# A two-layer gated attention and convolution trunk: scaling moved ahead of the weights' split, and one convolution tile moved from GpSimd to VectorE

## The reference

```
h = rmsnorm(x);  proj = h @ w_in            # 10 groups of columns
y_a = window_attention(q, k, v, sinks, bias) @ w_attn_out
c = ca * sigmoid(cb);  c = causal_dwconv(c, 31 taps) + bias
c = silu(layernorm(c));  y_b = c @ w_conv_out
y_c = (sc_b * causal_dwconv(sc_c * sc_h, 3 taps)) @ w_sc_out
x = x + (g0*y_a + g1*y_b + g2*y_c) @ w_mix_out      # g = sigmoid(gates)
x = x + (silu(h2 @ w_gate) * (h2 @ w_up)) @ w_down
x = x + (p @ w_ple) * sigmoid(rmsnorm(x) @ w_ple_gate)
```

## Time and profile before

| | us |
|---|---|
| median of 3 runs | 1161.26 (1160.84 to 1161.86) |
| the profiled execution, its time | 1161.75 |
| its span | 1160.0 |
| TensorE busy | 1121.8 (97%) |
| VectorE busy | 841.3 (73%) |
| ScalarE busy | 705.8 (61%) |
| GpSimd busy | 419.7 (36%) |
| mean granted clock of TensorE | 0.997 |

### The profile page before, as it was taken

The page is one execution under the profiler, slowest core; times in us unless marked ns, Lnnn a source line. Parts: engine busy times, 40 slices in busy tenths (PEclk is TensorE's granted clock), DMA queues, the critical chain, the costliest instruction groups (busy, mean ns, idle before and its releaser), DMA issues.

```text
span 1160.0 us, 24019 instructions
## 1 busy us (share of the span) xinstructions
PE 1121.8 (97%) x9244; PEld 1100.3 (95%) x9244; DVE 841.3 (73%) x1265; ACT 705.8 (61%) x1139; POOL 419.7 (36%) x405
## 2 busy tenths in 40 slices
PE   5999899999999999999999989999999999999996
PEld 5998789999999999999989988999999999999996
DVE  6888997877667655455898899878776676545557
ACT  5768987757555553444667798876574554434453
POOL 0587568883002000002228876778600200000012
PEclk9999999999999999999999999999999999999998
DMA  8565334454553555455335543345555535545531
GB/s 302 195 236 194 110 116 162 166 206 166 183 212 110 201 203 214 151 188 206 112 145 203 195 153 140 110 150 211 184 178 191 185 132 199 204 185 185 185 146 37
DMA packets 29357, 201.52 MB, mean 174 GB/s; under 512 B 3521, under 2 KB 3713, under 8 KB 5841
## 3 DMA queue, kind: packets, MB, share of 16 engines
q1 hardware_dynamic: 27648, 195.38, 47.4%
q0 software_dynamic: 1088, 4.74, 1.2%
q10 hardware_dynamic: 528, 0.15, 0.1%
HBM read 199.19 MB, written 3.69 MB: 175 GB/s over the span
## 4 chain that ended last, share of the span: by engine, by line
PE 62%; DVE 14%; POOL 11%; ACT 7%; issue 4%; DMA 2%; POOLq 0%; ACTq 0%; DVEq 0%; SPq 0%
PE bank L322 20%; PE bank L324 20%; PE bank L323 20%; POOL pacc L1308 10%; DVE w_lo L875 4%; ACT w_hi L538 3%; DVE probs L1052 2%; POOL sqsum L1321 2%; DMA w_raw<-in_wstream 1%; DVE zacc L1076 1%; ACT cprod L538 1%; DVE act_lo L879 1%; PE bank L359 1%; PE bank L360 1%; DVE probs L1026 1%
## 5 line engine op out<-in xcount | busy, mean ns | idle before, releaser
L322 PE MATMUL bank<-h_hi,w_hi 128*128 128x256 f32 x1856 | 531.1, 286 | 2.9 <-DVE h_lo L879 0.9
L323 PE MATMUL bank<-h_lo,w_hi 128*128 128x256 f32 x1856 | 525.0, 283 | 0.0
L324 PE MATMUL bank<-h_hi,w_lo 128*128 128x256 f32 x1856 | 524.9, 283 | 0.0
L875 DVE TENSOR_TENSOR w_lo<-w_raw,w_hi 128x2048 fp32r<-128x2048 f32 x183 | 429.6, 2350 | 99.6 <-ACT w_hi L538 99.2
L538 ACT ACTIVATE w_hi<-w_raw 128x2048 fp32r<-128x2048 f32 (+1 forms) x185 | 351.2, 1900 | 153.6 <-DMA w_raw<-in_wstream 114.8
L322 PEld LDWEIGHTS bank<-h_hi,w_hi 128*128 128x128 f32 x1856 | 355.7, 192 | 10.9 <-issue 5.9
L323 PEld LDWEIGHTS bank<-h_lo,w_hi 128*128 128x128 f32 x1856 | 355.9, 192 | 0.1
L324 PEld LDWEIGHTS bank<-h_hi,w_lo 128*128 128x128 f32 x1856 | 355.8, 192 | 0.0
L1308 POOL TENSOR_TENSOR pacc<-pacc,cprod 128x256 f32<-128x256 f32 x280 | 304.2, 1086 | 76.6 <-ACT cprod L538 38.8
L322 PE MATMUL bank<-act_hi,w_hi 128*128 128x256 f32 x1024 | 291.9, 285 | 4.5 <-DVE w_lo L922 2.9
L323 PE MATMUL bank<-act_lo,w_hi 128*128 128x256 f32 x1024 | 290.4, 284 | 0.0
(11 more groups left out here) (133 smaller groups left out, 813.2 us busy)
## 6 DMA issues: line engine op xcount, KB each, us to landing
w_raw<-in_wstream SPq DMA_DIRECT2D x183, 1024.0 KB, 4.8
rel_bias_rows<-rel_bias_by_distance POOLq DMA_DIRECT2D x1, 2560.0 KB, 19.0
bias<-rel_bias_rows POOLq DMA_DIRECT2D x1, 1536.0 KB, 10.7
xs<-in_x SPq DMA_DIRECT2D x2, 512.0 KB, 4.4
w_raw<-in_wstream SPq DMA_DIRECT2D x2, 512.0 KB, 7.9
out_y<-xs SPq DMA_DIRECT2D x4, 256.0 KB, 2.6
zacc<-in_p POOLq DMA_DIRECT2D x2, 256.0 KB, 4.5
prms<-in_prm SPq DMA_DIRECT2D x1, 328.0 KB, 10.5
```

Of the source, the lines that this page charges most:

```text
L322: nc.tensor.matmul(o, wh, hi, start=first, stop=False, skip_group_check=True)
L323: nc.tensor.matmul(o, wh, lo, start=False, stop=False, skip_group_check=True)
L324: return nc.tensor.matmul(o, wl, hi, start=False, stop=last, skip_group_check=True)
L875: nc.vector.tensor_tensor(w_lo[:, n % RING, :], w_raw[:, n % RAW_RING, :], f32(w_hi[:, n % RING, :]), ALU.subtract).then_inc(lo_ready, 1)
```

## The change

Four things change.

- `POOL_CONV` loses tile 6, which goes to `LATE_CONV` beside tile 7. GpSimd makes four tiles and VectorE four, two of them early and two late. The late tiles accumulate in the two halves of PSUM bank 5.
- VectorE makes six late taps in each chunk of attn_out in place of four, and seven in each of the first two chunks of sc_out, where it had none.
- ScalarE makes three products in a chunk of sc in place of six, all at the chunk's end; the 36 that are left of 124 go to the eight chunks of attn_out (31 of 155 before).
- In the attention loop of VectorE `denominators` and `scale_probs` of pair j stand at the end of chunk j, ahead of that chunk's `w_lo`, in place of the beginning of chunk j + 1, behind it.

```diff
--- before.py
+++ after.py
@@ -81,15 +81,15 @@
 REL = 2 * SEQ // 2 + CHUNK
 KEYS = P + CHUNK
 
-POOL_CONV = (0, 3, 4, 5, 6)
+POOL_CONV = (0, 3, 4, 5)
 EARLY_CONV = (1, 2)
-LATE_CONV = (7,)
+LATE_CONV = (6, 7)
 POOL_ADDS = CONV_WIDTH - 1
 POOL_STEPS = len(POOL_CONV) * POOL_ADDS
 PRODUCTS = len(POOL_CONV) * CONV_WIDTH
 PROD_RING = 4
-CGLU_TAPS, QKV_TAPS, ATTN_TAPS = 5, 5, 4
-CGLU_PRODUCTS, QKV_PRODUCTS, SC_PRODUCTS = 4, 4, 6
+CGLU_TAPS, QKV_TAPS, ATTN_TAPS, SC_TAPS = 5, 5, 6, 7
+CGLU_PRODUCTS, QKV_PRODUCTS, SC_PRODUCTS = 4, 4, 3
 
 
 def _tap_order():
@@ -150,7 +150,7 @@
         cv = sb("cv", [P, DT, CPAD + SEQ])
         pacc = sb("pacc", [P, SEQ])
         cprod = sb("cprod", [P, PROD_RING, SEQ])
-        cacc = {1: psum[5][:, 0:SEQ], 2: psum[5][:, SEQ:2 * SEQ], 7: psum[5][:, 0:SEQ]}
+        cacc = {1: psum[5][:, 0:SEQ], 2: psum[5][:, SEQ:2 * SEQ], 6: psum[5][:, 0:SEQ], 7: psum[5][:, SEQ:2 * SEQ]}
         mu = sb("mu", [P, SEQ])
         sq_last = [mu[:, :], sq[:, 1, :]]
 
@@ -700,7 +700,6 @@
                         exponentials(j)
                     if 0 <= j - 1 < QT:
                         copy_probs(j - 1)
-                    conv_products(before_sc + SC_PRODUCTS * j + SC_PRODUCTS // 2)
                     for s in (2 * j, 2 * j + 1):
                         t, kind = s // 3, s % 3
                         if kind == 0:
@@ -1102,15 +1101,15 @@
                 for j in range(C0["attn_out"] - C0["sc"]):
                     if j == 0:
                         dve.wait_ge(bias_ready, 2)
-                    if 0 <= j - 1 < QT:
-                        denominators(j - 1)
-                        scale_probs(j - 1)
                     if j < QT:
                         softmax(j)
                     if 0 <= j - 2 < QT:
                         low_attn(j - 2)
                     if j > 0:
                         branch_strips(j - 1)
+                    if j < QT:
+                        denominators(j)
+                        scale_probs(j)
                     after_chunk(C0["sc"] + j - 1)
                 branch_strips(C0["attn_out"] - C0["sc"] - 1)
                 low_sc(DT - 1)
@@ -1126,6 +1125,8 @@
                     nc.vector.tensor_tensor(qm[:, j, :], qm[:, j, :], part[:, j % 2, :], ALU.add).then_inc(mix_added, 1)
                     if j < VAR_AT - 1 or j > VAR_AT:
                         after_chunk(C0["sc_out"] + j - 1)
+                    if j < MEAN_AT - 1:
+                        taps(min(EARLY_TAPS + ATTN_TAPS * DT + SC_TAPS * (j + 1), len(DVE_TAPS)))
                     if j == MEAN_AT - 1:
                         dve.wait_ge(mu_ready, L + 1)
                         for t in range(DT):
```

## The result

| | before | changed |
|---|---|---|
| median, us | 1161.49 (1160.84 to 1161.86) | 1172.99 (1171.6 to 1175.1) |
| span of the profiled execution | 1160.0 | 1173.3 |
| its time | 1161.75 | 1175.1 |
| mean granted clock | 0.997 | 0.987 |

The changed kernel is slower, by a ratio of 1.0095 (95% interval 1.0083 to 1.0106), which is 11.5 us. The forecast was +4.6 us, 1165.9, with a range up to 1171.5. The direction was right and the time lies outside.

What follows compares the result with a forecast made beforehand. TensorE bounds the kernel (busy 1121.8 of 1160.0 us), with VectorE nearly full too in attention. 2 x (2.2 - 1.8 + 1.9) = +4.6 us on the profiled 1161.75 gives 1166.35, median 0.5 lower: 1165.9, range 1160.0 to 1171.5.

Steps and rivals of the forecast that it cites:

- Behind the mean nothing is lost: After the mean's matmul: VectorE's 3.0 us before subtracting the mean are partly done during the stall, so no added cost.
- (a): Attention's first chunk: scaling ahead of `w_lo` delays the second softmax and first value product, +2.2 us per layer.
- (b): Attention loop after the first chunk: VectorE falls from 8.67 to 8.3 us a chunk, fewer TensorE stalls, -1.8 us per layer.
- (d): Two late tiles on VectorE, taps into sc_out: the mean's matmul waits longer, +1.9 us per layer, bounds +1.4 and +4.0.
- (c): Half the products in attention, 36 left for attn_out: GpSimd takes 5.96 us a chunk there against TensorE's 5.75; costed at nothing.
- third rival: At the mean, GpSimd's last add stands behind `w_lo`, stall 1.8 us longer: 1169.5 us, chance 0.15.
- The first: Rival: all 3.1 us of loop stalls go and the first value product is no later: 1157.9 us, chance 0.12.
- The second: Rival: GpSimd is last, its tiles end 4.4 us later and the mean's matmul waits for it: 1170.9 us, chance 0.11.

Runs made afterwards that it cites:

- e12: The changed kernel with 24 unread matmuls ahead of the first value product and 24 ahead of the mean's matmul; 1166.83 us.
- e2: The changed kernel with the old order on VectorE (scaling in the next chunk, behind `w_lo`); 1167.24 us.
- e5: e2 with six products a chunk in attention, in two halves, so none is left for attn_out; 1165.11 us.
- e1: The kernel before with only the new order on VectorE (scaling ahead of `w_lo`); 1173.96 us.
- e7: e2 with six products a chunk in the last four chunks of sc, leaving 24 instead of 36 for attn_out; 1162.88 us.
- e8: e2 with the earlier late taps of e6 and the later products in sc of e7; 1155.22 us.
- e6: e2 with late taps moved forward: four in each of sc's last four chunks, six in each of attn_out, none in sc_out; 1159.19 us.
- e4: The changed kernel with 24 unread matmuls ahead of the mean's matmul; 1170.48 us.

## Why the prediction was wrong

**The step that failed is the sum itself**: a wait was priced at its own length. It had every wait in its place, but no term for what follows a long one. "Behind the mean nothing is lost", it says, and there 2.1 and 1.5 us were lost, behind the first value product 2.6 and 2.6. That missing term is 8.8 us of the profiled 13.3. The prediction read the granted clock of the stage before, 1.00, and kept it for a kernel in which it forecast waits twice as long. Behind the stage's own waits of up to 2.2 us the trace of before shows no low clock. But its first microseconds do show a slow TensorE behind waits of 8.0 and 2.9 us. The second of these, and two rows of the table by stretch:

```profile
PE bank L322 <- DVE w_lo L922: 2.9, 1, 2.9
...
13.00:14.00 1.00, 1.00 (x6) 1.00 (x6) 0.96 (x3) 1.00 (x2) 0.00 (x0) 1.00 0.03 12
...
22.00:23.00 1.00, 1.00 (x11) 1.00 (x10) 1.00 (x2) 0.00 (x0) 0.00 (x0) 1.00 1.05 321
```

There are 6 matmuls of a strip in 1 us, then 11, the same counts as at 0.50 and at 1.00 in the changed kernel. The granted clock is given as 1.00 in both rows, so here the count says more than the column: matmuls of the same shape start 0.21 us apart from 12.5 to 15.1 us and 0.12 apart from 15.3 us on. That is a first price for the missing term, an estimate from these rows: 15 matmuls from 12.18 to 15.29 us, 3.1 us in place of 15 x 0.12 = 1.8, so 1.3 us. The Trainium skill has the rule that was wanted (TensorE: Matmul & The Clock Gate, "Part 1: The HAM clock gate"): the array's clock is halved by default, and only activity releases it. The trace of the changed kernel agrees, with its 0.50 behind each of the four long waits. With the clock held up (e12) the kernel takes 1166.8, where the sum said 1165.9.

That these two are so close is luck in part. The terms were off in both directions and cancel: over both layers (a) was 0.9 us too high, (b) 2.6 too high and (d) 3.8 too low.

**(a), the first chunk**: right in mechanism and nearly in size, 1.75 and 1.71 against 2.2. VectorE waited for the exponentials and ran the second softmax one `w_lo` later, as the step had it. The rows of the changed kernel, for the earlier trace rows, end with the second softmax, which started at 113.68 before:

```profile
111.18 0.16 DVE L1040 TENSOR_TENSOR srec<-sden,ssum 128x4 f32<-128x4 f32 x1 [5.74 <-ACT probs L675]
...
112.94 2.81 DVE L874 TENSOR_TENSOR w_lo<-w_raw,w_hi 128x2048 fp32r<-128x2048 f32 x1
115.67 0.28 DVE L1023 CUSTOM_DVE_ANT_0 probs<-bank,bias 128x128 f32<-128x128 f32 x1
```

**(b), the loop**: named rightly as the place where time is gained, sized at -1.8 and measured at -3.1, its own lower bound. By the step's own numbers six times 8.3 - 8.13 are 1.0 us of stalls left, not 1.3, which would have made it -2.1. The rows show what was undervalued. VectorE's scalings in the changed kernel, for the earlier trace rows, and a piece of its timeline, for the earlier trace rows:

```profile
L1051 DVE TENSOR_SCALAR probs<-probs,smx x16: 278/308/767, 111.6 to 137.8; 128x128 f32<-128x128 f32 x8, 128x192 f32<-128x192 f32 x8
```

```profile
119.52 0.94 DVE L1051 TENSOR_SCALAR probs<-probs,smx 128x128 f32<-128x128 f32 x4
120.38 2.29 DVE L874 TENSOR_TENSOR w_lo<-w_raw,w_hi 128x2048 fp32r<-128x2048 f32 x1
...
124.67 0.41 DVE L1098 TENSOR_TENSOR prod<-bank,zacc 128x256 f32<-128x256 f32 x1
126.33 0.16 DVE L1040 TENSOR_TENSOR srec<-sden,ssum 128x4 f32<-128x4 f32 x1 [1.25 <-ACT probs L675]
```

Their median is 308 ns against 503: the four take 0.94 us, where the step had taken off only half of the excess. The new wait of 1.25 us in every third chunk, behind the one branch product, is there to the hundredth (1.25 at 126.33), and costs nothing, since VectorE is now faster than TensorE. The cause was put wrongly. The step gave a part of the gain to the order, and e2 and e5 show that the number of products alone decides whether the loop stalls. For the scalings themselves both count: from 103 to 178 us they keep VectorE busy for 14.9 us before and 14.9 in e5, 13.0 with three products alone (e2), 11.5 with the order alone (e1) and 8.0 with both. The loop of e2 runs without stalls all the same, so shorter scalings aren't what ended them; what in VectorE's round did wasn't taken apart.

**(c), half the products**: costed at nothing "because (d) ends later", and here lay the mistake in (d). The period of 5.96 us that the step worked out came true, 5.98 between ScalarE's roundings (it waits for GpSimd's adds for 12.4 us between 202 and 250, where it was 8.1). It was only judged by GpSimd's own end. It acts through ScalarE's rounding on VectorE, which does the taps; and by e7 GpSimd's adds act on `w_lo` beside that.

**(d), the late tiles**: the count of 5.75 + 1.7 us from the chunk's end to the mean's matmul was right, as e5's wait of 1.8 shows. With VectorE 2.0 late instead of 0.4 the term came to +4.0 and +3.6 in place of +1.9, within its bound of +4.0. The last tap ended 12.9 us behind the start of sc_out's first gate product (249.95 to 262.84), where 11.5 were forecast. The last add was not held up by `w_lo`: the two last sums took 1.50 together. So the third rival fell. The rule of the Trainium skill on the shared ports (SBUF — State Buffer, "Who interferes with whom") had been weighed at that add; it isn't contradicted, since the add was under way before the `w_lo` at 263.75, which took 2.81 us.

**The rivals.** The first, all stalls of the loop gone, happened in its first half and not in its second. The second was right that GpSimd sets the pace in attn_out and wrong on how. None had the clock.

## What to carry to other kernels

A wait of TensorE costs more than its length where it lets the clock fall: to waits of some 4 us add the low stretch behind them, here 1.3 to 2.7 us each (and in some executions 1.2 to a wait of 2), or fill the wait with matmuls that nobody reads. That gives back the low stretch and not the wait: e12 is still 5.0 us slower than the kernel before. When work is thinned out in one stage it lands in the next; ask there not only whether the engine that does it ends in time, but who waits in its queue and what that one makes for others. And run the parts of a change alone: here one part gave all the gain in the loop, another cost more than that, and the costs of the two parts alone (12.4 and 5.7 us) don't add up to that of both (11.5).

## What the runs showed of the hardware that was not expected

- Behind waits of 3.8 to 4.8 us TensorE's granted clock is 0.50 for up to some 6 us of work. It need not be low yet when the wait ends: behind the mean of layer 1 in the changed kernel the matmul starts at 837.85, the clock is still 1.00 from 838 to 839 us and 0.50 from 840 to 842.
- For shorter waits the length alone doesn't decide it in these runs. Behind the 2.2 us before the first value product the clock stayed at 1.00 in the kernel before, and behind the same 2.2 us in layer 0 of e5 it was 0.50 from 119 to 121. Behind 2.1 us it stayed at 1.00 in layer 0 of e8, and in that of e6 it was 0.50 from 118 to 121 us, and the second value product came 1.2 us later than in layer 1, 9.68 against 8.45. The same stretch stands in e7 (9.63 against 8.45) and is 1.2 us of the 3 by which it missed its forecast. It is also a likely reason why the changed kernel's four runs scatter by 3.5 us and the four of the kernel before beside them by 1.0: the slowest has a mean granted clock of 0.987, the fastest 0.991. That wasn't tested by itself.
- 24 additional matmuls a layer, in the wait at the mean, save 2.5 us (e4), and 48 in two waits a layer save 6.2 (e12 against the changed kernel).
- VectorE's scalings take a median of 503 ns in the kernel before and 308 in the changed one, where the shortest take 278 to 305. Each half of the change brings the median down by itself, to 310 ns with the order alone (e1) and 311 with three products alone (e2), and six products in the old order bring it back (492 in e5). The median hides what is left: the busy time of all of them in the stage falls from 14.9 us to 11.5 and 13.0 with one half, and to 8.0 with both.
